# A decoder layer on one core: value tiles from the turned input, and queries and keys from blocks normalised in place

## The reference

```python
def rms_norm(x, g):
    xf = x.astype(jnp.float32)
    y = xf * lax.rsqrt(jnp.mean(xf * xf, axis=-1, keepdims=True) + RMS_EPS)
    return (y * g.astype(jnp.float32)).astype(x.dtype)

hn = rms_norm(x, g_pre_mix)
proj = hn @ w_in
mq, mk, mv, fq, fk, fv, f_logit, cvb, cvc, cvh = jnp.split(proj, SPLIT_IDX, axis=-1)
# 6 block-sparse heads (mq, mk, mv), 6 forgetting heads (fq, fk, fv), a short convolution
mixed = concat(moba, fox, conv) @ w_out
x = x + rms_norm(mixed, g_post_mix)
h2 = rms_norm(x, g_pre_ffn)
ff = (silu(h2 @ w_gate) * (h2 @ w_up)) @ w_down
return x + rms_norm(ff, g_post_ffn)
```

## Time and profile before

| | |
|---|---|
| runs | 576.1, 575.08, 575.63 us |
| profiled execution | 576.57 us, span 574.8 us |
| granted clock over the span | 0.998 |
| TensorE busy | 567.5 us (99%) |
| VectorE / ScalarE / GpSimd busy | 471.5 (82%) / 319.7 (56%) / 110.4 us (19%) |
| DMA | 78.92 MB, mean 137 GB/s |

### The profile page before, as it was taken

How to read it: one execution, slowest core, us unless ns; L and a number is a source line. 1 busy time by engine, 2 the same in 40 slices (tenths; PEclk the granted TensorE clock), 3 DMA queues, 4 the chain that set the end, 5 groups by cost and what they waited for, 6 DMA issues and landing times.

```text
span 574.8 us, 9664 instructions
## 1 busy us (share of the span) xinstructions
PE 567.5 (99%) x3372; PEld 502.8 (87%) x3372; DVE 471.5 (82%) x791; ACT 319.7 (56%) x539; POOL 110.4 (19%) x129
## 2 busy tenths in 40 slices
PE   8999999999999999999999999999999999999996
PEld 6988888888888888899999999999999988888884
DVE  5647888888797954799888988988898788888787
ACT  5625765766555645575545546454554565547762
POOL 3020001103220000000324242332324002233100
PEclk9999999999999999999999999999999999999999
DMA  8274334346312471302323223242322359999743
GB/s 331 85 214 136 91 105 132 95 141 185 110 48 100 147 299 68 111 38 75 144 76 131 88 75 144 73 145 74 144 75 81 138 188 268 269 211 199 167 146 146
DMA packets 23144, 78.92 MB, mean 137 GB/s; under 512 B 2972, under 2 KB 2972, under 8 KB 23114
## 3 DMA queue, kind: packets, MB, share of 16 engines
q1 hardware_dynamic: 16716, 57.44, 28.2%
q0 software_dynamic: 6304, 21.00, 16.1%
q10 hardware_dynamic: 94, 0.09, 0.0%
HBM read 71.16 MB, written 4.22 MB: 131 GB/s over the span
## 4 chain that ended last, share of the span: by engine, by line
PE 99%; DVE 0%; POOL 0%; issue 0%; DVEq 0%; ACT 0%; POOLq 0%
PE bank L1666 11%; PE bank L1668 11%; PE bank L1667 11%; PE bank L1951 8%; PE bank L1950 8%; PE bank L1949 8%; PE bank L1957 7%; PE bank L2019 6%; PE bank L2017 6%; PE bank L2015 6%; PE bank L1960 3%; PE bank L1720 3%; PE bank L1827 3%; PE bank L1815 2%; PE bank L1805 1%; PE bank L1803 1%
## 5 line engine op out<-in xcount | busy, mean ns | idle before, releaser
L1950 PE MATMUL bank<-tok_lo,form_hi 128*128 128x256 f32 x320 | 90.6, 283 | 0.0
L1951 PE MATMUL bank<-tok_hi,form_lo 128*128 128x256 f32 x320 | 90.6, 283 | 0.0
L1949 PE MATMUL bank<-tok_hi,form_hi 128*128 128x256 f32 x320 | 90.5, 283 | 0.0
L1666 PE MATMUL bank<-hn,w_hi 128*128 128x512 f32 (+1 forms) x200 | 76.6, 383 | 0.0
L1668 PE MATMUL bank<-hn,w_lo 128*128 128x512 f32 (+1 forms) x200 | 75.0, 375 | 0.0
L1667 PE MATMUL bank<-hn,w_hi 128*128 128x512 f32 (+1 forms) x200 | 74.6, 373 | 0.0
L1949 PEld LDWEIGHTS bank<-tok_hi,form_hi 128*128 128x128 f32 x320 | 60.9, 190 | 1.9
L1951 PEld LDWEIGHTS bank<-tok_hi,form_lo 128*128 128x128 f32 x320 | 61.1, 191 | 0.0
L1950 PEld LDWEIGHTS bank<-tok_lo,form_hi 128*128 128x128 f32 x320 | 61.0, 191 | 0.0
L2015 PE MATMUL bank<-dw_hi,da_hi 128*128 128x512 f32 x154 | 59.9, 389 | 0.0
L2019 PE MATMUL bank<-dw_hi,da_lo 128*128 128x512 f32 x154 | 59.9, 389 | 0.0
(11 more groups left out here) (206 smaller groups left out, 1397.0 us busy)
## 6 DMA issues: line engine op xcount, KB each, us to landing
raw<-in_w_gate_units SPq DMA_DIRECT2D x22, 512.0 KB, 3.6
raw<-in_w_up_units SPq DMA_DIRECT2D x22, 512.0 KB, 4.5
raw<-in_w_in_units SPq DMA_DIRECT2D x21, 512.0 KB, 3.3
down_x<-in_w_down POOLq DMA_DIRECT2D x15, 512.0 KB, 9.7
down_y<-in_w_down SPq DMA_DIRECT2D x10, 512.0 KB, 9.2
raw<-in_w_out SPq DMA_DIRECT2D x8, 512.0 KB, 3.2
q_lh<-q_hl POOLq DMA_DIRECT2D x12, 256.0 KB, 2.8
down_x<-in_w_down SPq DMA_DIRECT2D x5, 512.0 KB, 3.9
```

What stands on the lines that cost most here:

```text
L1666: nc.tensor.matmul(out_ap, sh, mh, start=first, stop=False)
L1949: nc.tensor.matmul(out_ap, sh, mh, start=first and k == 0, stop=False, skip_group_check=True)
L1950: nc.tensor.matmul(out_ap, sh, ml, start=False, stop=False, skip_group_check=True)
L1951: mm = nc.tensor.matmul(out_ap, sl, mh, start=False, stop=k == HK - 1, skip_group_check=True)
```

## The change

The host now hands over the input a second time, turned (`x_t`, features on the partitions). Value tiles are made from x g, split into hi and lo block by block (`features_hi`, `features_lo`) straight from the turned input, for all four token tiles at once in four PSUM banks; the root is applied when they are read out of PSUM. The roots are still formed from the input in token order (`x_open`), spread along a row (`r_tok`), turned by four transposes (`row_scales`), and then the eight blocks are normalised in place (`normalise`) and split again (`tokens_hi`, `tokens_lo`) into the same `hn_hi`, `hn_lo`, for queries, keys and everything after. The 32 transposes of the input and the spreading of g go.

SyncE's order of loads, the chunks, and GpSimd's new work (all of the rounding of units 3 to 5, the rests of 4 and 5; `swap(0)` moves behind the first bias loads):

```diff
-V_CHUNKS = ((0, 2), (2, 5), (5, 8))
+V_CHUNKS = ((0, 1), (1, 4), (4, 8))
+X_CHUNKS = ((0, 2), (2, 4), (4, 8))
+LATE_CHUNK = 2
+POOL_UNITS = (3, 4, 5)
+POOL_RESTS = (4, 5)
...
+            load_turned(0)
             load_values(0)
             load_values(1)
+            load_turned(1)
             load_values(2)
-            load_open(2)
-            load_open(3)
+            load_turned(2)
             load(3, unit(w_in_units, 0))
-            load(4, unit(w_in_units, 1), 1)
+            for t in range(TT):
+                load_open(t)
+            load(4, unit(w_in_units, 1), 0)
...
+            nc.gpsimd.memset(r_tok[:, :, :], 1.0).then_inc(ones_set, 1)
...
             for u in range(V_UNITS):
+                if u == LATE_CHUNK:
+                    pool.wait_ge(tables_in, 32)
...
+            def rounded(u):
+
+                pool.wait_ge(raw_in[u % RAW], 16 * (u // RAW + 1))
...
+            def rest(u):
+
+                hi, lo = split_slot(u)
+                pool.wait_ge(pool_hi_done, POOL_UNITS.index(u) + 1)
+                nc.gpsimd.tensor_tensor(lo[:, :, :], staged(u), hi[:, :, :], ALU.subtract).then_inc(pool_lo_done, 1)
...
+            rounded(3)
+            rounded(4)
+            rest(4)
             pool.wait_ge(rel_copied, 2)
             pool.dma_start(rel_rows.ap(), rel_row[:, :]).then_inc(rel_out, 16)
+            rounded(5)
+            rest(5)
 
             for p in range(MOBA_PAIRS + 1):
                 load_bias(p)
-                if p >= 1:
-                    swap(p)
+                swap(p)
```

ScalarE:

```diff
+            def features_hi(k):
+
+                chunk = next(n for n, (k0, k1) in enumerate(X_CHUNKS) if k0 <= k < k1)
+                act_e.wait_ge(xt_in[chunk], 16)
+                nc.scalar.activation(hn_hi[:, k, :], xt[:, k, :], ACT.Copy, scale=g_feat[:, k:k + 1]
+                                     ).then_inc(hn_hi_done, 1)
...
+            def tokens_hi(k):
+
+                if k < KT - 1:
+                    act_e.wait_ge(v_used, k + 1)
+                else:
+                    act_e.wait_ge(proj_done, V_GROUPS[-1] + 1)
+                act_e.wait_ge(xn_done, k + 1)
+                nc.scalar.copy(hn_hi[:, k, :], xt[:, k, :]).then_inc(hn_hi_done, 1)
...
-            squares_of(0)
-            squares_of(1)
...
+            act_e.wait_ge(g_in, 16)
+            for k in range(KT):
+                features_hi(k)
+            for t in range(TT):
+                squares_of(t)
...
+            for k in range(KT):
+                tokens_hi(k)
             split(6)
-            evac_hi(group(0, 1))
-            evac_hi(V_GROUPS[3])
```

VectorE; `split(6)` and three value tiles move into the first attention steps:

```diff
+            def features_lo(k):
+
+                dve.wait_ge(hn_hi_done, k + 1)
+                nc.vector.scalar_tensor_tensor(out=hn_lo[:, k, :], in0=xt[:, k, :], scalar=g_feat[:, k:k + 1],
+                                               in1=hn_hi[:, k, :], op0=ALU.mult, op1=ALU.subtract
+                                               ).then_inc(hn_lo_done, 1)
...
+            def row_scales(t):
+
                 inverse_std(SQ1, t)
...
+                if t == 0:
+                    dve.wait_ge(ones_set, 1)
+                nc.vector.tensor_scalar(r_tok[:, t, :], r_tok[:, t, :], rstd[:, SQ1, t:t + 1], None, ALU.mult
+                                        ).then_inc(r_tok_done, 1)
+
+            def normalise(k):
+
+                if k == 0:
+                    dve.wait_ge(hn_lo_done, KT)
+                    dve.wait_ge(r_turned, 1)
+                nc.vector.scalar_tensor_tensor(out=xt[:, k, :], in0=xt[:, k, :], scalar=g_feat[:, k:k + 1],
+                                               in1=bank[:, R_BANK, :], op0=ALU.mult, op1=ALU.mult).then_inc(xn_done, 1)
+
+            def tokens_lo(k):
+
+                dve.wait_ge(hn_hi_done, KT + k + 1)
+                nc.vector.tensor_tensor(hn_lo[:, k, :], xt[:, k, :], hn_hi[:, k, :], ALU.subtract
+                                        ).then_inc(hn_lo_done, 1)
...
+                    src = bank[:, V_BANKS[p], :]
+                    for m in range(MOBA_PAIRS):
+                        last = nc.vector.scalar_tensor_tensor(
+                            out=v_moba[:, m, p, :, DH:P],
+                            in0=src[:, P * m:P * (m + 1)].rearrange("p (h d) -> p h d", h=2),
+                            scalar=rstd[:, SQ1, p:p + 1], in1=v_moba[:, m, p, :, 0:DH], op0=ALU.mult,
+                            op1=ALU.subtract)
+                    last.then_inc(v_lo_done, 1)
+                    nc.vector.tensor_scalar(f_tok[:, p, :], src[:, MOBA_W:V_COLS], rstd[:, SQ1, p:p + 1], None,
+                                            ALU.mult).then_inc(proj_read, 1)
...
+            features_lo(0)
             split(0)
...
+            features_lo(1)
+            split(1)
+            features_lo(2)
+            features_lo(3)
...
+            for k in range(4, KT):
+                features_lo(k)
             split(2)
...
+            split(3)
+            for t in range(TT):
+                row_scales(t)
+            normalise(0)
+            for k in range(KT):
+                if k + 1 < KT:
+                    normalise(k + 1)
+                tokens_lo(k)
+            evac_lo(group(0, 0))
+            evac_lo(group(0, 1))
             evac_lo(V_GROUPS[0])
...
+                if g == 0:
+                    split(6)
+                if g < TT - 1:
+                    evac_lo(V_GROUPS[g + 1])
```

TensorE:

```diff
+            def row_scales():
+
+                pe.wait_ge(r_tok_done, TT)
+                for t in range(TT):
+                    mm = nc.tensor.transpose(bank[:, R_BANK, P * t:P * (t + 1)], r_tok[:, t, :], ident[:, :])
+                mm.then_inc(r_turned, 1)
...
+                    wait_rest(pe, u)
+                    if G > TT + 1:
+
+                        pe.wait_ge(proj_read, reads_with(G - 2))
+                if G <= TT + 1:
+                    pe.wait_ge(hn_lo_done, KT + k + 1)
...
+            def v_weight_rests(u, ks):
+
+                pe.wait_ge(lo_done, u + 1)
+                for k in ks:
+                    for t in range(TT):
+                        mm = v_mm(t, k, hn_hi, wv_lo, False, k == KT - 1)
+                        if k == KT - 1:
+                            mm.then_inc(proj_done, 1)
+                    if k < KT - 1:
+                        mm.then_inc(v_used, 1)
...
+            for u in range(V_UNITS):
+                pe.wait_ge(wv_hi_done, u + 1)
+                for k in range(*V_CHUNKS[u]):
+                    pe.wait_ge(hn_hi_done, k + 1)
+                    for t in range(TT):
                         v_mm(t, k, hn_hi, wv_hi, k == 0, False)
...
+                    pe.wait_ge(hn_lo_done, k + 1)
+                    for t in range(TT):
+                        v_mm(t, k, hn_lo, wv_hi, False, False)
+                    if u < LATE_CHUNK:
+                        v_weight_rests(u, (k,))
             relative_rows()
-            v_token_rests(1)
-            v_weight_rests(0, [1, 2]).then_inc(proj_done, 1)
...
+            v_weight_rests(LATE_CHUNK, (4, 5))
+            row_scales()
+            v_weight_rests(LATE_CHUNK, (6, 7))
+            pe.wait_ge(rel_copied, 2)
+            proj_step(group(0, 0), V_UNITS, 0)
+            for k in range(1, KT):
+                proj_step(group(0, 0), V_UNITS, k)
+                if k >= 2:
+                    proj_step(group(0, 1), V_UNITS + 1, k - 2)
+            for k in range(KT - 2, KT):
+                proj_step(group(0, 1), V_UNITS + 1, k)
...
+                items = filler_at(g)
+                if g == 0:
+                    for G, k in items:
+                        proj_step(G, G - 1, k)
+                    items = []
                 logits_step(g)
...
-                if g == 1:
+                if g == 4:
                     forget_rows()
```

238 lines of the change are left out of this document (70 added, 168 removed).

## The result

The changed kernel took 582.63 us (median of 4 runs, 580.89 to 583.9) against 575.87 for the kernel before (4 runs): ratio 1.0114, 95% interval 1.0098 to 1.0129. It is 6.8 us slower. The forecast was 574.6 us with a range of 572.4 to 576.9: wrong in sign, and the time lies outside the range. The profiled execution took 583.9 us, the longest of the four, and its span is 582.2.

The account below looks back on a forecast made before the run. TensorE, busy 99% of the span, was taken as the bound. Gain 1.5 us at the second logits less 0.5 for VectorE's debt: profiled 576.57 to 575.6, median 574.6 us, range 572.4 to 576.9.

Parts of the forecast that it names:

- When the first value product can run: Start of the kernel: first value product at 5.8 us, bounds 5.2 and 6.9, set by the first weight chunk's landing and rounding.
- The value stretch: Value products on TensorE: no waits, fast from 9.6 us, root transposes from 24.1 to 24.5, roots 2.2 us ahead.
- The chain behind the roots: VectorE normalises blocks for the queries: first query product at 26.65, two more 0.65 us waits; price 2.1 us.
- From queries to logits: Query block to landed swap 6.05 us, TensorE waits 1.3; second logits 43.15 against 44.68, gain 1.5 us.
- What VectorE still owes: Readouts and split(6) around steps 0 to 2: 4.6 us of slack used up, 0.5 us lost, leaving gain 1.0.
- GpSimd's new work: Rounding and rests of units 4 and 5, then bias loads, on GpSimd: done before needed, all hidden.
- The rule on GpSimd's SBUF interface: GpSimd contends with VectorE's two-input SBUF reads; loss expected on GpSimd, possibly on VectorE's chain from 24.5 to 30.6 us.
- The rule on transposes and the clock: Transposes do not count as busy for TensorE's clock, so 12 warming transposes buy nothing; the rise hangs on value products.
- D: Rival, chance 0.12: dearer readouts or VectorE's chain slowed 30% beside GpSimd's rests; gain goes, 575.6 us within 0.3.
- E: Rival, chance 0.10: the swap's second half lands up to 7.5 us after issue instead of 3.1; 578.4 us.
- B: Rival, chance 0.25: TensorE fast sooner, at 7.3 us; gain 2.5, giving 573.1 us.
- A: The forecast itself, chance 0.35: the sum as predicted, own range 573.8 to 575.4 us.

Follow-up runs that it names:

- run 2: Changed kernel plus products nobody reads in TensorE's waits (12 ahead of the first query product, 3 each ahead of blocks 1 and 2): 580.77 us, ratio 1.0079.
- run 5: Changed kernel with both GpSimd weight-rest subtractions (units 4 and 5) moved to VectorE's idle times, GpSimd's order kept: 579.63 us, ratio 1.0078.
- run 6: The kernel of run 5 plus one useless GpSimd subtraction of two parts of x into an unread buffer: 581.19 us, ratio 1.0094.
- kernel 17: Changed kernel with only the warm-up transposes raised from 12 to 22: 582.70 us, ratio 1.0109.
- run 8: Changed kernel with the first weight chunk loaded ahead of x and split(0) ahead of the first rest: 583.19 us, ratio 1.0116.
- kernels 13: Kernel of run 5 with dummy products, key products four blocks behind queries', all four value tiles read out ahead of the keys: 576.88 us, ratio 1.0020.
- 14: As kernel 13, with the first weight chunk loaded ahead of x and split(0) ahead of the first rest: 576.53 us, ratio 1.0019.
- kernel 15: As kernel 13, with 22 warm-up transposes instead of 12: 576.24 us, ratio 1.0005.
- 16: As kernel 14, with 22 warm-up transposes instead of 12: 576.34 us, ratio 1.0008.
- run 3: Changed kernel with split(6) and value tiles 0 to 2 read out ahead of queries and keys on VectorE, all four on ScalarE: 579.34 us, ratio 1.0057.
- runs 1: Changed kernel with GpSimd's rounding and rest of unit 5 waiting until VectorE's chain of blocks is through: 585.0 us, ratio 1.0163.
- 4: Changed kernel with late unit 5 subtraction, added TensorE products (6 ahead of the first query product) and earlier value readouts together: 587.75 us, ratio 1.0199.

## Why the prediction was wrong

The profiled executions give the whole overrun. The forecast for this one was 575.6 us and it took 583.9, 8.3 us more. Stretch by stretch, in us:

| stretch | forecast | measured | too long | reason |
|---|---|---|---|---|
| start to VectorE's first block | 24.5 | 26.67 | 2.2 | first value product 1.5 late, the rest in the value stretch and the transposes |
| to the first query product | 2.15 | 3.80 | 1.65 | the lock, 1.5 |
| to the first logits | 16.25 | 17.51 | 1.3 | the clock |
| to the first product with the values | 16.6 | 19.74 | 3.1 | readout debt, and the clock |

The clock's share of the third row is read from kernels 2, 5 and 6, where this stretch took 16.3 us at a granted clock of 1.00. That of the fourth is read from kernels 5, 6 and 17, where it took 18.1 us at 1.00 against 19.7 at 0.83 (the changed kernel, 2 and 8); without readout debt it took 15.8 to 15.9 (kernels 13 to 16). So 2.3 us are the debt itself and 1.6 the clock behind it. The four rows give 8.2 of the 8.3 us.

- **When the first value product can run**: failed, 7.29 instead of 5.8. The bound of 6.9 was passed too. The weight chunk landed 0.95 us later than I put it (6.25 for 5.3). The rounding of 0.45 was priced alone; it took 0.99 beside a rest and 0.51 without (run 8).
- **The value stretch**: its mechanism was right. No waits in it, rise of the pace at 11.3 instead of 9.6, late chunk fast throughout. The root transposes began at 25.78 where the sum had 24.1, and were through near 26.5 instead of 24.5. The root itself was not 2.2 us ahead but 0.7: the last row scale was held until 25.06 by GpSimd (2.38 us).
- **The chain behind the roots**: this is the step whose mechanism failed first. "first query product at 26.65, 0.7 us after TensorE ran dry" was 30.47, 2.81 us after. Of these 3.8 us, 2.2 are the later start of VectorE's chain, 1.5 the lock and 0.1 the operations themselves. The later waits of 0.67 and 0.73 were as forecast. The clock that fell behind them was not in the sum (1.2 us here, though not in each execution).
- **From queries to logits**: held. From block to landed swap it took 5.9 us for 6.05, the swap itself 3.0 for 3.1, the wait at the first logits 1.33 for 1.3. Only all of it lay 5.1 us later.
- **What VectorE still owes**: failed, 0.5 forecast and 3.3 measured by the medians (run 3). The price of a readout was right (3 pieces in 0.87 and the column in 0.22, 1.0 together). The wrong path was walked: I followed VectorE's queue to the divided probabilities, which TensorE did not wait for at all. The queue also holds the readout of the next queries, whose bank a filler needs, and there the 2.46 us were lost.
- **GpSimd's new work**: "All hidden" was false, and with the readout debt it is the main fault. Its length (2.39 for 3.1 forecast) and its due times were right, and nobody waits for its result; it costs by running at all.
- **The rule on GpSimd's SBUF interface** was read by half and weighed too low. I took 30% on a chain for the worst case and gave it a share in a case of 0.12. The page of the Trainium skill, "GPSIMD Engine Reference", 1. Specifications, says that the two contend when VectorE reads two inputs from SBUF. This trace agrees and gives the size, 2.20 us instead of 0.68. The same line there also names instructions in a 2-port perf mode, which I left out; the row scale, one tensor and a scalar, was held as well (2.38 for 0.28), which fits it, though no run here shows the mode it ran in. The rule in full stands on another page of the Trainium skill, which I had not weighed, "SBUF — State Buffer", SBUF: two separate sides: the pair of ports is an exclusive lock, held for a whole instruction by whoever starts first, and VectorE takes it also with one input when it runs in a mode that uses two ports. The rows shown here agree. By it block 0's rest would have been priced at what was left of GpSimd's 2.35 us, 1.65, and its own 0.68: 2.3, measured 2.20. The rows of before showed it already on GpSimd's side, 1.52 against 1.17 us; I took it for a rate where it is a turn.
- **The rule on transposes and the clock**: with 22 instead of 12 the first 8 loads took 1.78, 1.74 and 1.37 us in the three profiled executions (runs 15 to 17), where with 12 it was 2.45 us in twelve and 1.36 to 1.38 in three. In kernel 17 the pace rose while only transposes had run. So the clock can rise on transposes alone, against the rule weighed in the prediction, and the measurement decides. How much the ten more of them did in each execution is not shown, since the 22 also shorten the idle time ahead of the first product, from about 2 us to 0.3 or less. What else differs between executions stays open.
- **The rivals**: D was the right family at a fraction of the price: it had 575.6, 1.0 us above the forecast, and the kernel came out 8.0 above it. E's price appeared in runs 1 and 4 only. B's faster rise came in some executions, not in this one. The 32 transposes did leave TensorE's queue; 0.35 for A rested on the cover being free.

Of the 6.8 us against the kernel before, medians give 3.0 to the lock and what follows it (run 5, loose), 3.3 to the readout debt with the clock behind it (run 3), and 1.9 to the clock (run 2); these overlap and do not add up.

The rest of the plan was sound. In kernel 15, with lock, readouts and start mended, the profiled execution passed the forecast's marks closely: first logits 43.5 for 42.9, first product with the values 59.3 for 59.5, 575.52 us for 575.6. That is partly luck, since it was the second fastest of eleven. Its median, 576.24, is not below the kernel before (575.89 on that chip), although its profiled span is 1.0 us shorter (573.8 against 574.8): this execution lies 0.7 us below its kernel's median, the profiled one of the kernel before (576.57) 0.7 above. So the forecast gain of 1 us is not shown by any kernel here, and what takes it back is open. That the query chain on VectorE costs what the transposes gave back is a guess.

## What to carry to other kernels

Before giving idle GpSimd work beside VectorE, list what VectorE runs in that time: an operation like the two held here, a subtraction of two SBUF inputs or a scaling of one, can be held until a GpSimd instruction has ended, and that costs even if nobody waits for GpSimd's result. When work is taken off the bounding engine, walk the queue of the next one to every buffer it must free, not only to the results it must deliver. A wait put into one queue to avoid a collision moves all that stands behind it, DMAs above all. And before a difference between two traces is given to a change, compare their starts and clocks: here they made 2.0 of 3.6 us in run 5 and 0.7 of 2.1 in run 6.

## What was not expected of the hardware

- Turns, not shares, between GpSimd and VectorE, and both ways: GpSimd's cast of 6 columns took 1.33 us beside VectorE's two-input subtraction (1.86 us at 9.55) where it took 0.18 before. VectorE's scaling operation with one of its inputs from PSUM was not slowed (1.41 us for two), its row scale from SBUF alone was.
- Executions of nearly the same program can run TensorE at 1.2 or 2.4 GHz through their first 4 to 6 us of products (kernels 13 and 14), a difference of 1.9 us at the late chunk. The granted clock in the profile's windows is 1.00 in both; only the pace of the loads shows it.
- The swap's two DMAs of 256 KB landed 3 us after issue alone and 7.1 us beside four bias loads of the same size in the same queue.
